# Attention scores of a two-layer decoder trunk as fp32r products of hi and lo parts, query parts stacked on the partitions

## The chip, the cores and the metric

The kernel runs on one core of one Trainium2 chip. The metric is the device time of one execution in microseconds (us), lower is better. "Before" and "after" are the same program but for the change below.

## What is computed

Two decoder layers on x of 256 tokens and 1024 channels. Each layer has a mixing part (this is where the change lies), a cross-attention into a memory of 256 rows, and a feed-forward part that reads 16384 single-neuron experts. Cut to what matters, the attention branch of the mixing part is, for 8 heads of 64 channels in 2 key/value groups of 4 heads:

```python
q = rms_norm(q, q_norm)                                   # (256, 8 heads, 64)
k_s = rms_norm(kv[:, :, 2], k_norm[1]); v_s = kv[:, :, 3] # "selected" branch, (256, 2 groups, 64)
k_w = rms_norm(kv[:, :, 4], k_norm[2]); v_w = kv[:, :, 5] # "window" branch
k_c, v_c = compressed(kv[:, :, 0:2])                      # 15 compressed keys and values per group
for each branch b in (c, s, w):
    o_b = masked_softmax(q @ k_b.T * 64 ** -0.5, causal) @ v_b
o = sum of sigmoid(gate_b) * o_b
```

With 256 tokens the selected and the window branch both see all causal keys, so both are plain causal attention with their own keys and values. Tokens come in two tiles of 128 (t = 0, 1); tile 0 sees 128 keys, tile 1 sees 256.

## The kernel before

**The stream.** All large weights come as "pieces" of 128 rows by 512 columns, 2 to a DMA, in one fixed order. ScalarE (ACT) rounds a piece to fp32r (`w_hi`, line 528), GpSimd (POOL) subtracts to get the rest (`w_lo`, line 494), and TensorE (PE) multiplies: `take(n)` on PE consumes n pieces, each with six fp32r matmuls of 512 columns (hi by hi, hi by lo, lo by hi, for two token tiles; lines 971 to 973). Four slots hold pieces: ACT may fill a slot only when PE has used the piece four before it (`hi(n)` on ACT, semaphore `used`), and POOL follows ACT. The small work of the attention, in plain fp32, is laid between the takes by hand; every engine has its own order written out, joined by semaphores.

**PSUM.** Four banks, `aux`, serve all small work. The list USES (line 90 on) says which use takes which bank in which order. PE waits in `wait_bank_free` for the engine that drains the use before it in that bank, and in `wait_drained` for a drained use; VectorE (DVE) or ACT wait in `wait_filled`.

**Attention.** The keys of both branches are normalised (`knd`), transposed (`kn_T0`, `kn_T1`) and written by DVE at line 1535 into `kTm` with zeros in the other head's half, so that one fp32 matmul gives the scores of a pair of heads; the zeros are four memsets (line 1446). The queries are normalised (line 1521), transposed in pairs of heads (`q_T0`, `q_T1`, 8 transposes in all) and written to `qT` (line 1543). A unit is (t, branch, pair): 16 units, first all of tile 0 and then all of tile 1. For unit u:

- PE `scores(u)`: one fp32 matmul, 256 columns (t = 0) or 512 (t = 1), line 1082. The profile shows an fp32 matmul as two records.
- DVE `unit_scores(u)`: scale and mask (line 1397 holds every `stt`), maximum (line 1615), signal `s_ready`.
- ACT: two exponentials with row sums (line 659), signal `p_exp`; then `hi(2)`, and at units 0, 4, 8 and 12 also `read_gates` (line 572).
- PE, in the loop over units: `take(1)`, wait `p_exp`, transposes `p_T{u}` (line 904; 2 or 4), `scores(u + 2)`, `take(1)`, wait for the drained `p_T{u}`, then 2 or 4 fp32 matmuls with the values (line 1115).
- DVE, in its loop: copy `p_T{u}` (line 1648), `unit_scores(u + 2)`; after every fourth unit `combine` scales the four heads' output by the gate over the sum (lines 1633 to 1640).

The compressed branch: `cmp_s` is eight fp32 matmuls of 32 columns (line 1094) between `scores(1)` and unit 0; DVE masks and exponentiates them in unit 0 (lines 1628, 1629, 1653 to 1655) until `pc_ready`; `oc0` and `oc1` (line 1127) follow in units 2 and 3. Before all this DVE makes the compressed keys: it waits for `cmp_k`, sums squares (line 1418 is the last, signal `kc_mean`), and ACT waits for `kc_mean` between two calls of `hi`.

## Time and profile before

| what | value |
|---|---|
| time, median of 3 runs | 2135.74 us (2135.69 to 2135.74) |
| the profiled execution: its own time | 2134.6 us |
| its span, first to last instruction | 2132.8 us |
| PE busy | 2119.8 us, 99% |
| POOL busy | 1709.4 us, 80% |
| DVE busy | 1227.5 us, 58% |
| ACT busy | 1188.5 us, 56% |
| granted TensorE clock | 1.000 over the whole span |

The trace is of one execution. Times in it count from the first instruction. The units of layer 0 lie at about 115 to 190 us, those of layer 1 about 1059 us later.

In a timeline a row has the start in us, how long until the end in us (for matmuls the end is modelled, and the next one starts before it), engine, line, operation, what it writes and reads, the shape, and how many are merged into the row.

### The profile page before, as it was taken

Reading aid. Unit: us, or ns where it says so; the run is one execution under the profiler, and the core shown is the slowest. Engines: PE = TensorE matmul, PEld = TensorE weight load, DVE = VectorE, ACT = ScalarE, POOL = GpSimd, SP = SyncE. Lnnn points to the kernel's source line nnn. Section 1 sums busy time; section 2 is a strip of 40 time slices with the busy share of each in tenths; the row PEclk is TensorE's granted clock in tenths of the full one; section 3 lists DMA queues with packets and bytes.
Section 4 is the critical chain, followed back from the end, with each engine's and each line's share of the span. In section 5 each row is a group of like instructions: output and inputs, shape, how many; then the busy total and the mean of one; then the engine's idle time right before and its main releaser. Section 6 shows DMA issues by size and latency. Waiting matters only on the chain.

```text
span 2132.8 us, 48901 instructions
## 1 busy us (share of the span) xinstructions
PE 2119.8 (99%) x14774; PEld 1842.0 (86%) x14774; DVE 1227.5 (58%) x2433; ACT 1188.5 (56%) x2287; POOL 1709.4 (80%) x1316
## 2 busy tenths in 40 slices
PE   9999999999999999999999999999999999999999
PEld 7878899999888888888878788999988888888887
DVE  5756448966666555423357564588665666553233
ACT  5555665555555545555555556655555555545565
POOL 7766678888788888888887576798888878888887
PEclk9999999999999999999999999999999999999999
DMA  8433445555544554565574344455555544555555
GB/s 293 157 124 129 147 149 176 179 177 178 166 158 167 168 172 163 196 196 188 188 257 149 123 132 139 154 180 185 178 168 167 167 166 161 173 170 197 189 192 180
DMA packets 101790, 367.87 MB, mean 172 GB/s; under 512 B 11600, under 2 KB 12880, under 8 KB 101456
## 3 DMA queue, kind: packets, MB, share of 16 engines
q1 hardware_dynamic: 97632, 354.46, 50.1%
q10 hardware_dynamic: 4080, 12.42, 1.5%
q8 instruction: 43, 0.70, 0.1%
q14 instruction: 35, 0.29, 0.0%
HBM read 365.78 MB, written 1.05 MB: 172 GB/s over the span
## 4 chain that ended last, share of the span: by engine, by line
PE 96%; DVE 1%; ACT 1%; issue 1%; POOL 1%; DMA 0%; ACTq 0%; DVEq 0%; POOLq 0%
PE acc L1215 11%; PE acc L1301 11%; PE acc L1303 11%; PE acc L1302 11%; PE acc L1205 6%; PE acc L1206 6%; PE acc L1207 6%; PE acc L971 6%; PE acc L973 5%; PE acc L972 5%; PE acc L1214 5%; PE aux L1259 4%; PE aux L904 2%; PE aux L1082 1%; PE aux L1115 1%
## 5 line engine op out<-in xcount | busy, mean ns | idle before, releaser
L494 POOL TENSOR_TENSOR w_lo<-raw,w_hi 128x512 fp32r<-128x512 f32 x1312 | 1709.2, 1314 | 415.6 <-ACT w_hi L528 321.2
L528 ACT ACTIVATE w_hi<-raw 128x512 fp32r<-128x512 f32 x1348 | 843.7, 629 | 651.7 <-PE acc L973 175.1
L1301 PE MATMUL acc<-w_hi,eg 128*128 128x512 f32 x1020 | 401.2, 393 | 0.0
L1303 PE MATMUL acc<-w_hi,eg 128*128 128x512 f32 x1020 | 397.6, 390 | 0.0
L1302 PE MATMUL acc<-w_lo,eg 128*128 128x512 f32 x1020 | 397.1, 389 | 0.0
L1944 DVE TENSOR_TENSOR eg<-big,eg 128x256 fp32r<-128x256 f32 x256 | 159.0, 621 | 398.3 <-ACT eg L785 396.5
L1215 PE MATMUL acc<-h_rows,w_hi 128*128 128x512 f32 x1024 | 355.8, 397 | 0.0
L1205 PE MATMUL acc<-h_rows,w_hi 128*128 128x256 f32 x1024 | 290.5, 284 | 0.0
L1206 PE MATMUL acc<-h_rows,w_hi 128*128 128x256 f32 x1024 | 289.9, 283 | 0.0
L1207 PE MATMUL acc<-h_rows,w_lo 128*128 128x256 f32 x1024 | 289.9, 283 | 0.0
L1214 PE MATMUL acc<-h_rows,w_lo 128*128 128x256 f32 x896 | 249.8, 279 | 0.0
L1303 PEld LDWEIGHTS acc<-w_hi,eg 128*128 128x128 f32 x1020 | 191.5, 188 | 40.5
L1302 PEld LDWEIGHTS acc<-w_lo,eg 128*128 128x128 f32 x1020 | 191.7, 188 | 38.9
L1301 PEld LDWEIGHTS acc<-w_hi,eg 128*128 128x128 f32 x1020 | 191.6, 188 | 38.5
L785 ACT ACTIVATE eg<-big 128x256 fp32r (+1 forms) x256 | 106.8, 418 | 204.4 <-PE acc L1303 204.3
L1215 PEld LDWEIGHTS acc<-h_rows,w_hi 128*128 128x128 f32 x1024 | 185.2, 188 | 33.8
L1205 PEld LDWEIGHTS acc<-h_rows,w_hi 128*128 128x128 f32 x1024 | 196.6, 192 | 0.5
L1207 PEld LDWEIGHTS acc<-h_rows,w_lo 128*128 128x128 f32 x1024 | 196.6, 192 | 0.0
L1206 PEld LDWEIGHTS acc<-h_rows,w_hi 128*128 128x128 f32 x1024 | 196.6, 192 | 0.0
L1214 PEld LDWEIGHTS acc<-h_rows,w_lo 128*128 128x128 f32 x896 | 168.8, 188 | 5.7
L1935 DVE TENSOR_REDUCE big<-acc 128x512 f32 (+1 forms) x128 | 88.5, 692 | 140.4 <-PE acc L1215 140.4
L971 PE MATMUL acc<-w_hi,h_rows 128*128 128x512 f32 x352 | 146.8, 417 | 4.5 <-POOL w_lo L494 1.8
(276 smaller groups left out, 2982.7 us busy)
## 6 DMA issues: line engine op xcount, KB each, us to landing
raw<-stream_dram SPq DMA_DIRECT2D x674, 512.0 KB, 3.3
big<-parb_dram ACTq DMA_DIRECT2D x2, 2128.0 KB, 10.3
big<-mem_dram ACTq DMA_DIRECT2D x2, 1024.0 KB, 5.3
big<-pm_dram ACTq DMA_DIRECT2D x2, 768.0 KB, 15.9
X<-x_dram ACTq DMA_DIRECT2D x1, 1024.0 KB, 8.5
out_dram<-X SPq DMA_DIRECT2D x4, 256.0 KB, 2.1
big<-parr_dram ACTq DMA_DIRECT2D x2, 448.0 KB, 12.0
big<-mem_dram ACTq DMA_DIRECT2D x1, 512.0 KB, 4.9
```

Source lines behind the costliest of these rows:

```text
L494: nc.gpsimd.tensor_tensor(w_lo[:, k % SLOTS, :], raw[:, k // PER_CHUNK, k % PER_CHUNK, :], w_hi[:, k % SLOTS, :].bitcast(F32), ALU.subtrac ...
L528: nc.scalar.activation(w_hi[:, k % SLOTS, :], raw[:, (k // PER_CHUNK) % RAW, k % PER_CHUNK, :], ACT.Copy).then_inc(hi_ready, 1)
L971: pe_.matmul(dst, r_hi[:, kt, ts], w_hi[:, slot, :], start=first, stop=False)
L1205: pe_.matmul(dst, wh, h_hi[:, kt, :], start=(kt == 0), stop=False)
L1206: pe_.matmul(dst, wh, h_lo[:, kt, :], start=False, stop=False)
L1207: return pe_.matmul(dst, w_lo[:, r % SLOTS, wk * P:(wk + 1) * P], h_hi[:, kt, :], start=False, stop=(kt == KD - 1))
L1214: pe_.matmul(acc[:, bank_of, 0:S], w_lo[:, r % SLOTS, at], h_hi[:, kt, :], start=False, stop=False)
L1215: ins = pe_.matmul(acc[:, bank_of, :], w_hi[:, r % SLOTS, at], h_rows[:, kt, :, :], start=(kt == 0), stop=(kt == KD - 1))
L1301: pe_.matmul(dst, eg[:, q % 2, 0, ts], w_hi[:, slot, :], start=start, stop=False)
L1302: pe_.matmul(dst, eg[:, q % 2, 0, ts], w_lo[:, slot, :], start=False, stop=False)
L1303: ins = pe_.matmul(dst, eg[:, q % 2, 1, ts], w_hi[:, slot, :], start=False, stop=stop)
L1944: V.tensor_tensor(eg[:, q % 2, 1, :], src, eg[:, q % 2, 0, :].bitcast(F32), ALU.subtract).then_inc(sig["eg_ready"].sem, 1)
```

## The change

- **Score products.** A unit is now one head with both branches: (g, t, q) for group g, tile t, head q of the group; first all of group 0, then group 1. The query of a head stands twice on the partitions: rows 0 to 63 its fp32r rounding, rows 64 to 127 the rest (`q_ring`, a ring of four). The keys stand twice too, once as rounding and once as rest (`k_parts`). Two fp32r matmuls of 256 or 512 columns then give the sum of all four products. The second token tile of group 1's keys (`k_late`) takes the place of group 0's only after unit 8 (`k_made`).
- **Queries.** Normalised per tile (two instructions in place of one), doubled by ACT (`zq_twice`, two copies of 512 columns), transposed per head (16 transposes in four uses `q_T0` to `q_T3` in place of 8 in two), written to `q_rows` (four instructions in place of two). Per unit DVE makes the parts with `unit_query`: a copy of 128 by 128 and a subtraction on 64 rows. Four are made ahead of `cmp_k`, the others in the loop.
- **Keys.** Per branch three products and two subtractions in place of two products; no zero halves, so the four memsets go.
- **Compressed scores.** Sixteen fp32 matmuls on 64 rows and 16 columns, even heads into one bank and odd into another, in place of eight on 128 rows and 32 columns; DVE drains them with four instructions in place of two.
- **Combination.** Per group and tile, both branches at once; the sum into `ot` becomes two additions of 256 columns where it was one of 512.
- **Banks and order.** The list of bank uses is rearranged, and the query transposes move to four places between the takes.

```diff
+         ("q_T0", 1), ("hid_p", 2), ("pool_d0", 0), ("pool_d1", 3), ("hid", 2), ("zg", 1), ("q_T1", 0), ("cmp_k", 2), ("cmp_v", 3),
+         ("q_T2", 1), ("q_T3", 0), ("mixed", 1), ("pool_y", 0), ("kc_T", 2), ("cmp_s0", 3), ("cmp_s1", 2)]
+UNITS = [(t, g, q) for g in range(KVG) for t in range(T) for q in range(GROUP)]
...
+        q_ring = k_blocks[:, 3, :].rearrange("p (u j) -> p u j", u=4)
...
# ACT, after zg_parts
+                a.wait("qn_ready")
+                for t in range(T):
+                    a.step(nc.scalar.activation(zq_twice[t][:, :, 1, :], zq_twice[t][:, :, 0, :], ACT.Copy), "q_twice" if t else None)
                 hi(2)
...
# PE
                 take(1)
-                e.wait("qn_ready")
-                for i in range(2):
-                    transposes(f"q_T{i}", [zq[:, t, j * P:(j + 1) * P] for j in (2 * i, 2 * i + 1) for t in range(T)])
+                def queries_T(i):
+                    transposes(f"q_T{i}", [zq_twice[t][:, h, :, :].rearrange("p n c -> p (n c)")
+                                           for h in (2 * i, 2 * i + 1) for t in range(T)])
                 take(2)
+                e.wait("q_twice")
+                queries_T(0)
...
                 fill(ins, "zg")
-                take(4)
+                take(2)
+                queries_T(1)
+                take(2)
...
                 fill(pe_.matmul(bank("cmp_v")[:, 0:DK], hid_rep, w2[:, 1, :], start=True, stop=True), "cmp_v")
-                take(4)
+                queries_T(2)
+                take(2)
+                queries_T(3)
+                take(2)
...
                 def scores(u):
+                    e.wait("q_made", u + 1)
+                    if (g, t, q) == (1, T - 1, 0):
+                        e.wait("k_made")
                     e.wait_bank_free(f"s{u}")
-                    fill(pe_.matmul(bank(f"s{u}")[:, 0:2 * w], qT[:, j, t * P:(t + 1) * P], kTm[:, br, j // 2, :, 0:w],
-                                    start=True, stop=True), f"s{u}")
+                    for n in range(2):
+                        keys_at = k_parts[:, n, :, 1 - g:2 - g + t, :]
+                        ins = pe_.matmul(bank(f"s{u}")[:, 0:2 * w], q_ring[:, u % 4, :], keys_at, start=(n == 0), stop=(n == 1))
+                    fill(ins, f"s{u}")
...
+                    for h in range(8):
+                        half = slice((h % 2) * DK, (h % 2 + 1) * DK)
+                        at = t * 64 + (h // 2) * 16
+                        ins = pe_.matmul(bank(f"cmp_s{h % 2}")[:, at:at + 16], q_rows[half, h, t * P:(t + 1) * P],
+                                         kc_rows[half, h // GROUP, :], start=True, stop=True)
...
# DVE
-                for br in range(2):
-                    for h in range(2):
-                        d.step(V.memset(kTm[(1 - h) * DK:(2 - h) * DK, br, :, h, :], 0.0))
...
+                    for g, c in ((0, slice(0, 2)), (1, slice(0, 1))):
+                        src = v[:, g].rearrange("p (c j) -> p c j", c=2)[:, c, :]
+                        hi, lo = (k_parts[:, n, br, 1 - g:1 - g + c.stop, :] for n in range(2))
+                        d.step(V.tensor_scalar(hi, src, gain, None, ALU.mult))
+                        d.step(stt(lo, src, gain, hi.bitcast(F32), ALU.mult, ALU.subtract))
+                    d.step(V.tensor_scalar(k_late[:, br, :], v[:, 1, P:2 * P], gain, None, ALU.mult), drains=use)
+                def query_rows(i):
+                    use = f"q_T{i}"
+                    d.wait_filled(use)
+                    d.step(V.tensor_scalar(q_rows[:, 2 * i:2 * i + 2, :], ..., col[:, C_QN:C_QN + 1], None, ALU.mult), drains=use)
+                def unit_query(u):
+                    t, g, q = UNITS[u]
+                    src, dst, low = q_rows[:, GROUP * g + q, t * P:(t + 1) * P], q_ring[:, u % 4, :], slice(DK, P)
+                    d.step(V.tensor_copy(dst, src))
+                    d.step(V.tensor_tensor(dst[low], src[low], dst[low].bitcast(F32), ALU.subtract), "q_made")
+                query_rows(0)
...
# after the copies of pool_d0 and pool_d1, ahead of cmp_k
+                query_rows(1)
+                for u in range(4):
+                    unit_query(u)
                 d.wait_filled("cmp_k")
...
                        "kcd_ready")
+                query_rows(2)
+                query_rows(3)
...
                     if u + 2 < len(UNITS):
                         unit_scores(u + 2)
+                    if u + 4 < len(UNITS):
+                        unit_query(u + 4)
+                    if u == len(UNITS) // 2:
+                        hi, lo = (k_parts[:, n, :, 1, :] for n in range(2))
+                        d.step(V.tensor_copy(hi, k_late))
+                        d.step(V.tensor_tensor(lo, k_late, hi.bitcast(F32), ALU.subtract), "k_made")
...
+                    for br in range(2):
+                        d.step(V.tensor_tensor(dst, dst, tmp[:, t, br * S:(br + 1) * S], ALU.add), done if br else None)
```

## Rows read from the trace of the kernel before

**Rows 1.** The page: shares of the chain that ended last, by engine.

```profile
PE 96%; DVE 1%; ACT 1%; issue 1%; POOL 1%; DMA 0%; ACTq 0%; DVEq 0%; POOLq 0%
```

**Rows 2.** Windows, the units of layer 0: busy us and instructions per engine, granted clock.

```profile
115.20:188.00 72.80, 72.74 (x377) 57.57 (x377) 37.87 (x73) 41.25 (x106) 41.11 (x32) 1.00 0.35 116
```

**Rows 3.** Timeline of PE: an fp32 score product of each width, and the stream behind.

```profile
119.50 0.60 PE L1082 MATMUL aux<-big 128*128 128x256 f32 x2
...
120.17 0.40 PE L972 MATMUL acc<-w_lo,eg 128*128 128x512 f32 x1
...
121.34 0.55 PE L1115 MATMUL aux<-big 128*128 128x64 f32 x4
...
144.93 1.02 PE L1082 MATMUL aux<-big 128*128 128x512 f32 x2
...
146.02 0.39 PE L972 MATMUL acc<-w_lo,h_rows 128*128 128x512 f32 x1
```

**Rows 4.** Timeline of PE, fp32r products of 256 columns, feed-forward stage, ten apart.

```profile
320.12 0.28 PE L1207 MATMUL acc<-h_rows,w_lo 128*128 128x256 f32 x1
...
321.32 0.28 PE L1205 MATMUL acc<-h_rows,w_hi 128*128 128x256 f32 x1
```

**Rows 5.** Timeline of PE: the eight query transposes, and the stream behind them.

```profile
86.64 1.04 PE L904 MATMUL aux<-cst,big 128*128 128x128 f32 x8
...
87.75 0.39 PE L972 MATMUL acc<-w_lo,eg 128*128 128x512 f32 x1
```

**Rows 6.** Timeline of PE: compressed scores on 128 rows; key products on 64 rows.

```profile
116.10 1.87 PE L1094 MATMUL aux<-big 128*128 128x32 f32 x16
117.81 0.47 PE L971 MATMUL acc<-w_hi,eg 128*128 128x512 f32 x1
...
309.50 2.06 PE L1244 MATMUL aux<-big 64*128 64x128 f32 x32
311.49 0.39 PE L1205 MATMUL acc<-h_rows,w_hi 128*128 128x256 f32 x1
```

**Rows 7.** Three DVE lines with all inputs in SBUF: duration ns min/median/max.

```profile
L1520 DVE TENSOR_TENSOR big<-big,st x8: 461/1397/1399, 79.0 to 1141.4; 128x256 f32<-128x256 f32 x8
L1480 DVE COPY big<-big x4: 1401/1402/1403, 61.9 to 1122.4; 128x512 f32<-128x512 f32 x4
L1640 DVE TENSOR_TENSOR big<-big x8: 691/1130/1295, 137.5 to 1253.1; 128x512 f32<-128x512 f32 x8
```

**Rows 8.** Timeline of DVE, units 0 and 1, and of PE: values of unit 1.

```profile
118.08 0.62 DVE L1397 SCALAR_TENSOR_TENSOR big<-aux,cst 128x128 f32<-128x128 f32 x2 [1.25 <-PE aux L1094]
...
120.55 0.42 DVE L1648 COPY big<-aux 128x256 f32<-128x256 f32 x1
...
122.90 0.73 DVE L1655 TENSOR_SCALAR st<-st 128x16 f32<-128x16 f32 x1
123.75 0.42 DVE L1648 COPY big<-aux 128x256 f32<-128x256 f32 x1
...
125.31 0.55 PE L1115 MATMUL aux<-big 128*128 128x64 f32 x4
```

**Rows 9.** Timeline of POOL: the second piece of unit 0.

```profile
122.31 1.29 POOL L494 TENSOR_TENSOR w_lo<-raw,w_hi 128x512 fp32r<-128x512 f32 x1 [0.18 <-ACT w_hi L528]
```

**Rows 10.** Timeline of DVE, then ACT, ahead of the units: keys, the mean, the next pieces.

```profile
87.54 3.10 DVE L1535 TENSOR_SCALAR big<-aux,col 64x512 f32<-64x512 f32 x4
...
101.25 0.14 DVE L1418 TENSOR_SCALAR st<-st 32x1 f32<-32x1 f32 x1
...
105.64 1.67 ACT L528 ACTIVATE w_hi<-raw 128x512 fp32r<-128x512 f32 x3
109.64 0.63 ACT L528 ACTIVATE w_hi<-raw 128x512 fp32r<-128x512 f32 x1 [2.32 <-PE acc L973]
```

**Rows 11.** Timeline at the end of the units: the last addition; PE's next transposes.

```profile
194.04 1.29 DVE L1640 TENSOR_TENSOR big<-big 128x512 f32<-128x512 f32 x1
...
196.22 1.03 PE L904 MATMUL aux<-cst,big 128*128 128x128 f32 x8
```

More of the change, by code:

```diff
@@ L91 @@
 USES += [("mk_T0", 0), ("mk_T1", 1), ("zg_p", 2), ("raw_T0", 0), ("raw_T1", 1), ("kn_T0", 3), ("kn_T1", 0),
-         ("q_T0", 1), ("q_T1", 2), ("hid_p", 3), ("zg", 3), ("hid", 2), ("pool_d0", 0), ("pool_d1", 1), ("cmp_k", 2), ("cmp_v", 3),
-         ("mixed", 0), ("pool_y", 1), ("kc_T", 2), ("cmp_s", 3)]
-UNITS = [(t, br, j) for t in range(T) for br in range(2) for j in range(PAIRS)]
+         ("q_T0", 1), ("hid_p", 2), ("pool_d0", 0), ("pool_d1", 3), ("hid", 2), ("zg", 1), ("q_T1", 0), ("cmp_k", 2), ("cmp_v", 3),
+         ("q_T2", 1), ("q_T3", 0), ("mixed", 1), ("pool_y", 0), ("kc_T", 2), ("cmp_s0", 3), ("cmp_s1", 2)]
+GROUP = 4
+UNITS = [(t, g, q) for g in range(KVG) for t in range(T) for q in range(GROUP)]
 USES += [("s0", 0), ("s1", 1)]
@@ L1089, in _ @@
                 e.wait_drained("kc_T")
-                e.wait_bank_free("cmp_s")
+                e.wait_drained("q_T3")
+                e.wait_bank_free("cmp_s0")
+                e.wait_bank_free("cmp_s1")
                 for t in range(T):
-                    for j in range(PAIRS):
-                        at = t * P + j * 32
-                        ins = pe_.matmul(bank("cmp_s")[:, at:at + 32], qT[:, j, t * P:(t + 1) * P], KcB[:, j // 2, :, :],
-                                         start=True, stop=True)
-                fill(ins, "cmp_s")
-                for u, (t, br, j) in enumerate(UNITS):
+                    for h in range(8):
[3 more added lines that the diff above has]
+                                         kc_rows[half, h // GROUP, :], start=True, stop=True)
+                        if t == T - 1 and h >= 6:
+                            fill(ins, f"cmp_s{h % 2}")
+                for u, (t, g, q) in enumerate(UNITS):
                     if u == len(UNITS) - 1:
@@ L1102, in _ @@
                     e.wait("p_exp", u + 1)
-                    transposes(f"p_T{u}", [sring[:, u % 2, h, c * P:(c + 1) * P] for h in range(2) for c in range(t + 1)])
+                    transposes(f"p_T{u}", [sring[:, u % 2, br, c * P:(c + 1) * P] for br in range(2) for c in range(t + 1)])
                     if u + 2 < len(UNITS):
@@ L1107, in _ @@
                     e.wait_drained(f"p_T{u}")
-                    use = f"o{u // PAIRS}"
-                    if j == 0:
+                    use = f"o{u // GROUP}"
+                    if q == 0:
                         e.wait_bank_free(use)
-                    for h in range(2):
+                    for br in range(2):
                         for c in range(t + 1):
-                            at = (2 * j + h) * DK
-                            g = j // 2
-                            ins = pe_.matmul(bank(use)[:, at:at + DK], pT[:, u % 2, h * (t + 1) + c, :],
+                            at = (GROUP * br + q) * DK
+                            ins = pe_.matmul(bank(use)[:, at:at + DK], pT[:, u % 2, br * (t + 1) + c, :],
                                              zkv[:, c, 3 + 2 * br, g * DK:(g + 1) * DK], start=(c == 0), stop=(c == t))
-                    if j == PAIRS - 1:
+                    if q == GROUP - 1:
                         fill(ins, use)
@@ L1442, in _ @@
                 rows_norm(ssx, X, xn, "xn_ready")
-                for br in range(2):
-                    for h in range(2):
-                        d.step(V.memset(kTm[(1 - h) * DK:(2 - h) * DK, br, :, h, :], 0.0))
                 halves = ident.rearrange("p (c a n) -> p c a n", c=2, a=2)
@@ L1629, in _, with combine, combine_group @@
                 d.step(V.tensor_tensor(scf, scf, cmb, ALU.subtract), "cs_ready")
-                def combine(use, t, k, weights, first, done=None):
+                def combine(use, shares, weights, dst):
                     d.step(V.reciprocal(coef, weights))
-                    d.step(stt(coef, ng[:, t, k:24:3], 1.0, coef, ALU.add, ALU.mult))
+                    parts = coef if len(shares.shape) == 2 else coef.rearrange("p (b q) -> p b q", b=2)
+                    d.step(stt(parts, shares, 1.0, parts, ALU.add, ALU.mult))
                     d.wait_filled(use)
-                    dst = (ot if first else tmp)[:, t, :].rearrange("p (h c) -> p h c", h=8)
-                    d.step(V.tensor_tensor(dst, bank(use).rearrange("p (h c) -> p h c", h=8),
+                    d.step(V.tensor_tensor(dst.rearrange("p (h c) -> p h c", h=8), bank(use).rearrange("p (h c) -> p h c", h=8),
                                            coef.unsqueeze(2).broadcast_to((P, 8, DK)), ALU.mult), drains=use)
-                    if not first:
-                        d.step(V.tensor_tensor(ot[:, t, :], ot[:, t, :], tmp[:, t, :], ALU.add), done)
+                def combine_group(n, done):
+                    g, t = n // T, n % T
+                    shares = ng[:, t, 3 * GROUP * g:3 * GROUP * (g + 1)].rearrange("p (q k) -> p k q", k=3)[:, 1:3, :]
+                    combine(f"o{n}", shares, sums[:, n % 2, :], tmp[:, t, :])
+                    dst = ot[:, t, g * GROUP * DK:(g + 1) * GROUP * DK]
+                    for br in range(2):
+                        d.step(V.tensor_tensor(dst, dst, tmp[:, t, br * S:(br + 1) * S], ALU.add), done if br else None)
                 unit_scores(1)
                 d.wait_drained("zg")
-                for u, (t, br, j) in enumerate(UNITS):
+                for u, (t, g, q) in enumerate(UNITS):
                     use = f"p_T{u}"
```

88 lines of the change are left out of this document (40 added, 48 removed).

## The prediction, made before the changed kernel was built or timed

> **What bounds the kernel now.** I read the page first: PE is busy for 99% of the span, and the chain that ended last is PE for 96% [rows 1]. Then the stretch of the change itself, the units of layer 0: PE is busy in 72.74 of 72.80 us at a granted clock of 1.00 (2.4 GHz), while DVE works 37.87, ACT 41.25 and POOL 41.11 us [rows 2]. So PE sets the end here, every us that PE is spared is gained, and every us that it is made to wait is lost, as nothing later gives it back. The other engines have 30 us of room in 73, which says little: what counts is whether DVE has each single thing ready when PE comes for it. A busy sum of PE does not price an instruction, since matmuls overlap in the records; I use distances from start to start.
>
> **What it removes from PE.** Behind an fp32 score product of 256 columns the take's second matmul starts 0.67 us after the product's start, behind one of 512 columns 1.09 us [rows 3]. One stream matmul lies between, which costs 0.234 (from 120.17 to 121.34 are five of them [rows 3]). So the products cost 0.67 - 0.23 = 0.43 and 1.09 - 0.23 = 0.86 us. The new ones are two fp32r products each. One of 512 columns is the stream's own kind, 0.23; one of 256 columns costs 0.120 (ten in 1.20 us [rows 4]). A unit of tile 0 then takes 0.24 in place of 0.43, one of tile 1 0.46 in place of 0.86. Eight of each per layer: 8 x 0.19 + 8 x 0.40 = 4.7 us less.
>
> **What it adds to PE.** Eight query transposes more per layer. Eight of them cost 87.75 - 86.64 - 0.23 = 0.88 us [rows 5]; I price four groups of four like two of eight. So 0.9 us more. Compressed scores: eight fp32 matmuls (16 records) took 117.81 - 116.10 = 1.71 us on all rows; 16 on half the rows, even and odd heads by turns as here, took 311.49 - 309.50 = 1.99 us for 32 records in the feed-forward part [rows 6]. The columns are fewer (16 against 128), but the 128 weight columns are the same. I take 0.1 more. Bounds: nothing, and, if the two halves did not run side by side, another 1.7. Values and probability transposes keep their number and size. Net on PE: -4.7 + 0.9 + 0.1 = -3.7 us per layer, if nobody waits.
>
> **What it adds to DVE, and why that is the question.** The trace shows DVE held up by POOL. L1520 has 256 columns and takes 0.46 us at best and 1.40 in the median, L1480 (a copy of 512) 1.40 each time, L1640 (512) 0.69 at best and 1.30 at worst [rows 7]. L1655 works on 16 columns and takes 0.73 us, until 123.63; POOL's subtraction ended at 123.60 [rows 8, 9]. So a DVE instruction whose inputs are all in SBUF, copy, scaling or two-input, may wait for POOL's running subtraction of 1.3 us; then, when POOL has the next piece ready, each of a row of them waits again. Copies and scalings from PSUM in the same stretch do not (0.42 at 120.55 and 123.75 [rows 8]). The added instructions are of the first kind: `unit_query` is an SBUF copy (about 0.22) and a subtraction of 128 columns (about 0.29; both estimates go by 0.42 for 256 columns less the part that grows), 16 times per layer, each up to 1.3 longer; `k_made` is two more, and the second addition in `combine` one more.
>
> The Trainium skill (SBUF — State Buffer, Who interferes with whom) says the same more sharply: the port pair that DVE and GpSimd share is an exclusive lock, taken by fp32 copies in SBUF and by two SBUF inputs, not by a reduction or a lone input outside such a mode. The trace agrees (1.40 against 0.46 in L1520). Were the rule idle here, the sum would be the first rival's.
>
> Now the places in order.
>
> *Ahead of the units.* DVE's work on the keys, 3.10 us for four [rows 10], becomes per branch two instructions of 256 and three of 128 columns from PSUM, some 0.48 and 0.35 each (0.75 for 512 columns, 0.42 for 256 as a copy), so 4.3 us: 1.2 later. `pool_d0` waits for the bank that this drains; in between PE has two more pieces but four fewer transposes. I count 0.2 there, and 0.1 at the bank that `q_T1` takes from `pool_d0`; bounds 0 and 1.5. ACT's two copies (0.63 each, as for a piece) fall where ACT runs ahead. The four `unit_query` before `cmp_k` take 2.3 us alone, and two or three of the eight meet a subtraction, so `kc_mean` comes at about 104.5 in place of 101.4 [rows 10], and the pieces that ACT makes behind it are up to 3.1 late. The three at 105.64 are followed by 2.32 us in which ACT waited for PE [rows 10], and PE comes 0.9 later by its transposes: 3.2 of room. Cost about 0.1.
>
> *Units 0 and 1.* DVE has no gap from 118.08 to the copy at 120.55 [rows 8], and PE starts unit 0's values at 121.34 [rows 3]: the copy had 0.37 us of room. Now PE is there 0.38 earlier after `scores(0)`, 0.19 more after `scores(2)`; DVE drains the compressed scores with four instructions of half the size in place of two of 0.31, +0.4, but starts 0.38 earlier. Wait about 0.3. Then `unit_query(4)` goes in front of the mask products and L1655. POOL's two pieces of unit 0 lie right there (122.31 to 123.60 [rows 9]), so its two instructions take about 1.7 in place of 0.5. Copy 1 came at 123.75 and PE used it at 125.31 [rows 8], 1.1 of room; DVE is now 1.7 later by this while PE arrives 0.5 sooner, net of the first wait. Wait about 1.0; bounds 0 and 2.2.
>
> *Unit 3.* Two combinations meet, and group 0's next units are of tile 1, so masks are 512 wide. `unit_query(7)`, the two additions and the 0.69 copy of `p_T4` end some 0.2 after PE asks; up to 2 if POOL stands in the way. Units 7, 8 (with `k_made`) and 11 have 0.5 us or more left. `k_made` itself is asked for two units later.
>
> *End of the units.* The last addition ran 194.04 to 195.33, and PE came at 196.22 [rows 11]. Two additions of 256, each behind a subtraction of POOL, end at about 196.5: 0.3.
>
> Waits per layer: 0.4 + 0.3 + 1.0 + 0.2 + 0.3 = 2.2 us. Memsets: they end before DVE waits for products of PE, and the way to the mix rows then goes over ACT; 0.
>
> **Sum.** (-3.7 + 2.2) = -1.5 per layer, -3.0 for two. The profiled execution took 2134.6 us by its own time (1.8 more than its span), 1.1 below the median of the runs; the difference applies to either. 2135.74 - 3.0 = 2132.7; with the rounding of the parts I say 2132.6 us, 0.15% faster, which a measurement of this kernel (about 0.2%, 4.3 us) can hardly tell from no change.
>
> **Rivals.**
> 1. *The waits are hidden* (0.25). DVE's small instructions fit between POOL's, or the room at the copies is enough. For it: only 41 of 73 us of POOL are taken in the units [rows 2]. Against: the copy of unit 0 had 0.37 us of room and loses more. Then 2 x -3.7: 2128.3.
> 2. *DVE feeds ACT too late* (0.08, the other side). All eight instructions of the four early `unit_query` wait a full subtraction, 10.4 in place of 2.3 us; `kc_mean` comes at 110, ACT holds back the pieces behind it, POOL too, and PE starves for about 5 us, beside the waits counted. 2 x (-3.7 + 2.2 + 5.1) = +7.2: 2142.9. It eats all gain from a delay of the mean of about 7 us on. Against: POOL has only some four pieces to do there, for ACT that waits gives it none, so the holding ends by itself. A milder form, 1 to 3 us per layer here or along the units, gives 2134.5 to 2139 (0.12).
> 3. *Halves of the array do not overlap* for products so short (0.05): +3.4 on the forecast, 2136.0. Against: rows 6.
> 4. *The parts are no cheaper* (0.02): two fp32r products with three-dimensional keys cost what one fp32 product did. Then +1.0 + 2.2 per layer: 2142.1.
>
> **Chances.** The forecast (2130.2 to 2134.5) has 0.48; a third of it lies below 2131.5. Faster by over 0.2%: 0.25 + 0.15 = 0.40. Slower by over 0.2%: 0.08 + 0.02 = 0.10. The rest, 0.50, within. The range takes in rival 1 with its own spread and the milder form of 2 and rival 3: 2128.0 to 2137.5; the forecast's own is 2130.2 to 2134.5.
>
> **What would show it.** Start to start, a score product and its stream matmul should take 0.47 (tile 0) and 0.69 (tile 1) in place of 0.67 and 1.09. The copies of line 1648's successor in units 0 and 1 should end after PE's take, with PE idle 0.3 and 1.0 us before the values and DVE named as releaser; `unit_query` pairs should show durations near 1 us where POOL is busy and 0.2 to 0.3 elsewhere. The distance from `zg_p` to the last query transposes should grow by no more than 2 us. The units of a layer should shrink by about 3 us. I am wrong if PE's idle before values is nil (rival 1), if POOL's subtractions or ACT's pieces come after PE asks in the takes behind `cmp_v` (rival 2), or if the compressed scores take over 2.5 us (rival 3).

## The result, and the profile after

The changed kernel takes 2142.66 us (median of 7 runs, 2141.61 to 2144.83) against 2135.69 for the kernel before on the same chip: ratio 1.0035, 95% interval 1.0025 to 1.0044. It is slower by 7.0 us, where 3.1 less were forecast. The profiled execution took 2142.09 us with a span of 2139.4.

The page of the changed kernel, its busy line and the shares of its chain, to be held against [rows 1]:

```profile
PE 2118.5 (99%) x14822; PEld 1840.0 (86%) x14822; DVE 1263.5 (59%) x2521; ACT 1191.4 (56%) x2291; POOL 1706.8 (80%) x1316
...
PE 90%; DVE 7%; issue 1%; ACT 1%; POOL 0%; DMA 0%; ACTq 0%; DVEq 0%; POOLq 0%
```

DVE had 1% of the chain and has 7%, though it works only 59% of the time. The busy line of PE says 99% in both kernels and does not tell them apart.

The stretch of the units, from the first score product to the last values of layer 0, in windows: first the kernel before, then the changed one. Columns: window, its length, busy us with instructions for PE, PEld, DVE, ACT and POOL, granted clock, DMA share, GB/s.

```profile
115.24:189.84 74.60, 74.54 (x387) 59.13 (x386) 38.96 (x75) 42.07 (x107) 41.91 (x33) 1.00 0.35 117
```

```profile
117.52:192.29 74.77, 71.86 (x403) 57.64 (x402) 53.88 (x106) 42.10 (x107) 41.79 (x33) 1.00 0.35 118
```

PE's busy time fell by 2.7 us and the stretch grew by 0.2, at the same granted clock of 1.00. DVE works 14.9 us more. PE's work did get shorter; it is now idle for 2.9 us, which is all that it saved and a little more. The waits in 115 to 215 us of the changed kernel name the places (engine and line that waits, releaser: us in total, times, longest):

```profile
PEld aux L1139 <- DVE big L1687: 4.4, 5, 1.6
...
PE aux L1139 <- DVE big L1687: 2.0, 2, 1.2
...
PEld aux L913 <- DVE big L1679: 0.6, 1, 0.6
PEld acc L980 <- DVE big L1421: 0.6, 1, 0.6
PE acc L980 <- DVE big L1421: 0.4, 1, 0.4
PE aux L913 <- DVE big L1669: 0.6, 2, 0.3
```

L1139 is the product with the values, L1687 the copy of `p_T` ahead of it, L913 the transposes, L1669 the draining product of a combination, L1679 its two additions, L1421 every `stt`, here that of the gates. The kernel before has one wait for DVE of 0.2 us in the units. Unit 1 on DVE, where [rows 8] had the copy at 123.75:

```profile
124.39 0.30 DVE L1574 CAST h_rows<-big 128x128 fp32r<-128x128 f32 x1
124.73 1.28 DVE L1575 TENSOR_TENSOR h_rows<-big,h_rows 64x128 fp32r<-64x128 f32 x1
126.04 0.43 DVE L1698 TENSOR_TENSOR big<-big,cst 128x256 f32<-128x256 f32 x1
...
126.96 0.78 DVE L1700 TENSOR_SCALAR st<-st 128x16 f32<-128x16 f32 x1
127.77 0.43 DVE L1687 COPY big<-aux 128x256 f32<-128x256 f32 x1
```

The subtraction of `unit_query(4)` ended at 126.01; a pair of POOL's pieces ran from 123.32 to 125.85. Counted from the first score product of each kernel (115.24 and 117.52), the copy comes 1.7 us later than before. Then unit 3, the largest wait of all, on DVE:

```profile
138.22 0.23 DVE L1574 CAST h_rows<-big 128x128 fp32r<-128x128 f32 x1
138.48 0.29 DVE L1575 TENSOR_TENSOR h_rows<-big,h_rows 64x128 fp32r<-64x128 f32 x1
138.80 0.20 DVE L1665 RECIPROCAL st<-st 128x8 f32<-128x8 f32 x1
139.04 1.14 DVE L1421 SCALAR_TENSOR_TENSOR st<-big,st 128x8 f32<-128x8 f32 x1
140.21 0.69 DVE L1669 TENSOR_TENSOR big<-aux,st 128x512 f32<-128x512 f32 x1
...
141.18 0.17 DVE L1421 SCALAR_TENSOR_TENSOR st<-big,st 128x8 f32<-128x8 f32 x1
...
142.11 1.84 DVE L1679 TENSOR_TENSOR big<-big 128x256 f32<-128x256 f32 x2
143.99 0.69 DVE L1687 COPY big<-aux 128x512 f32<-128x512 f32 x1
```

and on POOL and PE at the same time:

```profile
138.86 1.29 POOL L499 TENSOR_TENSOR w_lo<-raw,w_hi 128x512 fp32r<-128x512 f32 x1 [1.24 <-ACT w_hi L533]
141.92 1.29 POOL L499 TENSOR_TENSOR w_lo<-raw,w_hi 128x512 fp32r<-128x512 f32 x1 [1.76 <-ACT w_hi L533]
```

```profile
141.05 0.63 PE L913 MATMUL aux<-cst,big 128*128 128x128 f32 x4 [0.29 <-DVE big L1669]
...
144.73 1.10 PE L1139 MATMUL aux<-big 128*128 128x64 f32 x8 [1.20 <-DVE big L1687]
```

`unit_query(7)` itself takes an undisturbed 0.52. But it pushes the 8-column `stt` of the combination to 139.04, just behind the start of POOL's piece (138.86 to 140.15), and the `stt` ends at 140.18: 1.14 us for 8 columns, while the next one, at 141.18, where POOL stands still, takes 0.17. The transposes of `p_T4` wait for the bank behind it, and the values of unit 4 for a copy that stands behind two combinations and two additions. Unit 1 shows the cost of an instruction held up; unit 3 that of a small one shifting its neighbours.

The trace split by stages gives a ledger. Each number is how much longer PE takes between two of its instructions than between the same two in the kernel before (starts paired by their order). "Ahead" runs from 75.0 us of the kernel before to the first score product, "units" to the last values, "end" to the stream behind the next transposes (200.06), "merges" to 350.12; then three of these for layer 1. The first column, up to 75.0 us, is mostly the scatter of single executions: in the three runs that leave this part's code as before, e7, e8 and e11, it is -0.03, -0.72 and +0.93, and the largest, +3.33 of e10, belongs to an execution that took 2.6 us more than the median of its runs. A share of it that the change causes is not excluded for the other runs.

```
                           to 75 | layer 0: ahead  units   end  merges | layer 1: ahead  units   end
changed kernel             +0.62 |          +1.67  +0.17  +1.03  +0.34 |          +1.67  +0.17  +1.02
e1  no unit_query          +0.25 |          +1.70  -3.83  +1.01  +0.39 |          +1.63  -3.95  +1.03
e2  unit_query last        +0.63 |          +1.63  -2.31  +1.03  +0.47 |          +1.67  -2.43  +1.01
e3  fp32 product           +0.60 |          +1.71  +3.77  +1.03  +0.45 |          +1.66  +3.61  +1.03
e4  first four late        +0.64 |          +1.19  +0.19  +1.01  +0.39 |          +1.18  +0.16  +1.01
e5  additions deferred     +0.31 |          +1.63  -3.11  +1.03  +0.42 |          +1.64  -3.24  +1.02
e6  reordered              +0.39 |          +1.18  -3.07  +0.84  +0.39 |          +1.18  -3.20  +0.84
e7  old + unit_query       -0.03 |           0.00  +1.31   0.00  +0.10 |           0.00  +1.24   0.00
e8  old + reductions       -0.72 |           0.00  +0.80   0.00  +0.06 |           0.00  +0.78   0.00
e9  three addends          +0.74 |          +1.19  -3.07  +0.88  +0.39 |          +1.17  -3.23  +0.81
e10 keys first             +3.33 |          +2.61  -2.73  +0.88  +0.07 |          +2.61  -3.23  +0.81
e11 old, two additions     +0.93 |           0.00  +1.14  +1.04  +0.07 |           0.00  +1.12  +1.01
e12 copy of part moved     +1.35 |          +1.17  -3.11   0.00  +0.38 |          +1.18  -3.23   0.00
e13 one addition           +0.18 |          +1.63  -0.83   0.00  +0.11 |          +1.63  -1.00  +0.03
e14 neither                +0.15 |          +1.66  -4.09  +0.01  +0.04 |          +1.70  -4.23   0.00
e15 spread                 +1.66 |          +1.18  -4.09  +0.01  +0.33 |          +1.19  -4.20   0.00
```

The two layers agree within 0.2 us everywhere but in the units of e10 (0.5): what happens here repeats with the order of the instructions and is hardly chance.

### The profile page after: what moved, and what is told of

It reads as the page before. It is cut to its first block, busy times and chain, and to the rows that moved or that the text cites. A ratio compares the mean times of both kernels' runs of the same rounds, so it can differ in the third digit from the quotient of the medians.

```text
span 2139.4 us, 49129 instructions
## 1 busy us (share of the span) xinstructions
PE 2118.5 (99%) x14822; PEld 1840.0 (86%) x14822; DVE 1263.5 (59%) x2521; ACT 1191.4 (56%) x2291; POOL 1706.8 (80%) x1316
## 3 DMA queue, kind: packets, MB, share of 16 engines
HBM read 365.78 MB, written 1.05 MB: 171 GB/s over the span
## 4 chain that ended last, share of the span: by engine, by line
PE 90%; DVE 7%; issue 1%; ACT 1%; POOL 0%; DMA 0%; ACTq 0%; DVEq 0%; POOLq 0%
PE acc L1239 11%; PE acc L1325 11%; PE acc L1327 11%; PE acc L1326 11%; PE acc L1229 6%; PE acc L1230 6%; PE acc L1231 6%; PE acc L1238 5%; PE aux L1283 4%; PE acc L980 4%; PE acc L982 4%; PE acc L981 4%; PE aux L913 2%; PE acc L940 1%; PE aux L1139 1%
## 5 line engine op out<-in xcount | busy, mean ns | idle before, releaser
L1988 DVE TENSOR_TENSOR eg<-big,eg 128x256 fp32r<-128x256 f32 x256 | 150.7, 589 | 406.1 <-ACT eg L794 404.3
```

The costliest lines, as they stand in the source:

```text
L1988: V.tensor_tensor(eg[:, q % 2, 1, :], src, eg[:, q % 2, 0, :].bitcast(F32), ALU.subtract).then_inc(sig["eg_ready"].sem, 1)
```

## The experiments

My theory was that DVE's added small instructions wait for POOL, or push others behind it, and PE waits for DVE. Against it stood: PE's own new work costs more than priced; the loss lies ahead of the units; ACT is fed late (the prediction's rival 2). Each run was timed beside the kernel before; the ratio is to that, with its 95% interval.

### e1, e2, e3, e4: which part of the change costs

e1 leaves out `unit_query` from unit 4 on:

```diff
-                    if u + 4 < len(UNITS):
-                        unit_query(u + 4)
```

> Leaves out the 12 pairs of unit_query from unit 4 on (the score products then read old query parts; PE, ACT and POOL do the same work). Theory, DVE's small SBUF instructions are pushed behind POOL's subtractions and PE waits for what follows them: the waits of about 4.2 us per layer inside the units go, the two additions of each combination and what is late ahead of the units stay, so 2142.7 - 2 x 3.5 = about 2135.7 us (2134 to 2138), and the 8-column instruction of combine falls from 1.13 back to about 0.2 us in units 2 and 3. Rival, the loss lies in PE's own new work or in the stages ahead of the units: within 1 us of 2142.7.

Measured 2133.55 us, 0.9991 [0.9982, 1.0000]: 9.1 less than the changed kernel, 2 below the theory's figure and just below its range. The units fell by 4.0 and 4.1 us; ahead and end did not move. The three 8-column `stt` of units 2 and 3 take 0.17 us each here, as expected.

e2 moves the same two lines behind the combinations, at the end of a unit:

> The same DVE instructions, but unit_query comes at the end of each unit, behind the combinations, in place of ahead of them. Theory: the waits for bank 2 at units 2, 3 and 4 (0.18, 0.46 and 0.45 us per layer) go, as combine's 8-column instruction stands again where POOL is idle; the waits for the copies of units 1 and 4 (0.97 and 1.35) stay about as they are, since the sum of DVE's work between two copies is the same. So about 1 to 1.5 us per layer, 2140.0 us (2139 to 2141.5). Rival, only the amount of DVE's work counts and not its place: 2142.7 within 0.5. Rival, the copy suffers more as unit_query now stands right ahead of it: 2144 or more.

Measured 2138.06 us, 1.0018 [1.0009, 1.0027], 4.6 less than the changed kernel with the same instructions, and 0.9 below the expected range. The three waits for bank 2 went as expected, and that of unit 1 too, which I had expected to stay; that of unit 4 stayed and grew from 1.35 to 1.68. DVE in e2, at the place of unit 1:

```profile
124.37 0.49 DVE L1696 TENSOR_TENSOR big<-big,cst 128x256 f32<-128x256 f32 x1
...
125.35 0.69 DVE L1698 TENSOR_SCALAR st<-st 128x16 f32<-128x16 f32 x1
126.08 0.23 DVE L1574 CAST h_rows<-big 128x128 fp32r<-128x128 f32 x1
126.34 0.29 DVE L1575 TENSOR_TENSOR h_rows<-big,h_rows 64x128 fp32r<-64x128 f32 x1
126.66 0.42 DVE L1687 COPY big<-aux 128x256 f32<-128x256 f32 x1
```

The same work between the same two copies now ends 1.1 us earlier, since the pair starts between two of POOL's pieces (one ends at 126.01, the next starts at 126.41). The idea that only the sum between two copies counts was wrong: the order changes the sum.

e3 makes the scores one fp32 product and leaves the keys' low parts out:

```diff
-                    for n in range(2):
-                        keys_at = k_parts[:, n, :, 1 - g:2 - g + t, :]
-                        ins = pe_.matmul(..., q_ring[:, u % 4, :], keys_at, start=(n == 0), stop=(n == 1))
+                    keys_at = k_parts[:, 0, :, 1 - g:2 - g + t, :].bitcast(F32)
+                    ins = pe_.matmul(..., q_ring[:, u % 4, :].bitcast(F32), keys_at, start=True, stop=True)
```

> Each unit's scores are one fp32 product (query parts against the keys' high parts, the keys' low parts left out) in place of two fp32r products; all else stays. Prediction's price of the parts: 8 x 0.19 + 8 x 0.40 = 4.7 us per layer more of PE, of which the units where PE waits for DVE now take back up to 4; theory: +5 to +8 us, 2148 to 2151 us. Rival, the parts are no cheaper than the fp32 product: 2142.7. Rival, the gain was all swallowed by waits at DVE (PE's speed does not matter in the units): also near 2143.

Measured 2150.16 us, 1.0070 [1.0057, 1.0084], 7.5 more than the changed kernel; in the units +3.6 and +3.4 of the 4.7 priced. So the cheaper products are worth most of their price even beside the waits, and rival 4 falls.

e4 puts the first four `unit_query` behind `query_rows(3)`:

> The four early unit_query come behind query_rows(3), not ahead of the compressed keys. Theory (units hold most of the loss): bank 1 comes free earlier for the mixed product, where PE now waits some 0.4 us, and kc_mean returns from 105.0 to about 101.5 us; 0.3 to 0.6 us per layer, 2142.7 - 0.9 = 2141.8 us (2141 to 2142.7). Rival 2 of the prediction in its milder form, ACT held back by the late kc_mean is what costs: 2 us per layer or more, 2138.7 or below.

Measured 2141.22 us, 1.0029 [1.0018, 1.0040], 1.4 less. Ahead of the units 0.48 us per layer came back, where `mixed` (L1079) had waited for the bank that `query_rows(2)` drains; that wait is gone in e4. The mean of the compressed keys was ready 2.8 us earlier, but it was no feeding of ACT that came back: in the changed kernel ACT waited 2.00 us for the mean of the compressed keys, and still had 1.62 us in which it waited for PE:

```profile
105.19 0.20 ACT L659 ACTIVATE st<-st 32x1 f32<-32x1 f32 x1 [2.00 <-DVE st L1442]
...
111.92 0.63 ACT L533 ACTIVATE w_hi<-raw 128x512 fp32r<-128x512 f32 x1 [1.62 <-PE acc L982]
```

### e7, e8, e11: one added cost at a time, in the kernel before

e7 adds to the kernel before, at the place of `unit_query`, only

```diff
+                    if u + 4 < len(UNITS):
+                        qs, qd = qT[:, u % 4, 0:P], spare[:, u % 4, :]
+                        d.step(V.tensor_copy(qd, qs))
+                        d.step(V.tensor_tensor(qd[DK:P], qs[DK:P], qd[DK:P].bitcast(F32), ALU.subtract))
```

> The kernel BEFORE with 12 idle pairs per layer at the place where the changed kernel has unit_query: a copy of 128 columns and a subtraction of 128 columns on half the rows, into a buffer that nobody reads. Nothing else of the change. Theory (DVE's small two-sided SBUF instructions wait for POOL's subtractions, and PE then waits for DVE): PE is slower in these units by 4.7 us per layer than in the changed kernel, so less is late, but about 2.5 us per layer remain, 2135.2 + 5 = 2140 us (2138 to 2142), with pairs of 0.3 to 1.3 us. Rival, DVE has room for them and the loss has its cause elsewhere in the change: 2135.2 to 2136.

e8 has two `tensor_reduce` of 128 columns there instead:

> The kernel BEFORE with 12 pairs of idle reductions per layer at the same place, 128 columns each, about 0.29 us each and so 0.58 for a pair against 0.52 for an undisturbed unit_query. Theory, the waiting for POOL is what costs and a reduction of one input does not wait: each takes its 0.3 us also beside a running subtraction, and the time stays within 1 us per kernel of the kernel before, 2135.2 to 2136.5 us. Rival, the amount and number of DVE's instructions is what costs: as much as the run with the copies and subtractions.

Measured: e7 2138.16 us, 1.0015 [1.0006, 1.0024]; e8 2137.44 us, 1.0010 [1.0001, 1.0019]. Per layer 1.3 and 0.8 us in the units. So e7 lost half of the figure that I expected, at the lower edge of its range, and e8 more than I allowed: its expectation fell. The groups by line (busy us, mean ns) show that the reductions themselves never waited (all at 0.29), while some copies and subtractions did (0.23 and 0.29 alone); first e7, then e8:

```profile
L1654 DVE CAST h_rows<-big 128x128 fp32r<-128x128 f32 x12 | 4.8, 398 | 0.4
L1655 DVE TENSOR_TENSOR h_rows<-big,h_rows 64x128 fp32r<-64x128 f32 x12 | 4.5, 377 | 0.4
```

```profile
L1653 DVE TENSOR_REDUCE st<-big 128x1 f32<-128x128 f32 x12 | 3.4, 286 | 0.4
L1654 DVE TENSOR_REDUCE st<-big 128x1 f32<-128x128 f32 x12 | 3.4, 286 | 0.4
```

But the reductions shifted what follows them. In e8 the mask product of unit 0 started beside POOL's piece (121.60 to 122.89), and the 16-column instruction beside the next:

```profile
121.53 0.29 DVE L1654 TENSOR_REDUCE st<-big 128x1 f32<-128x128 f32 x1
121.85 1.32 DVE L1657 TENSOR_TENSOR big<-big,cst 128x256 f32<-128x256 f32 x1
...
123.66 1.12 DVE L1659 TENSOR_SCALAR st<-st 128x16 f32<-128x16 f32 x1
124.82 0.42 DVE L1648 COPY big<-aux 128x256 f32<-128x256 f32 x1
```

0.58 us of work that is never held made the copy late by more than a microsecond, through its neighbours. But e8's loss is 0.6 of e7's, so the two runs alone do not tell how much of e7's comes from instructions held themselves and how much from shifted ones. The Trainium skill (SBUF — State Buffer, Who interferes with whom) says that a reduction never contends on this chip, and an instruction with two inputs in SBUF does while GpSimd reads SBUF; the trace agrees (the reductions at 0.29 on the mean, the subtraction of e7 at 0.29 alone and 1.34 at worst), and the rule alone would have called e8 harmless.

e11 cuts each addition of a combination in the kernel before into two of 256 columns:

```diff
-                        d.step(V.tensor_tensor(ot[:, t, :], ot[:, t, :], tmp[:, t, :], ALU.add), done)
+                        for n in range(2):
+                            cs = slice(n * S, (n + 1) * S)
+                            d.step(V.tensor_tensor(ot[:, t, cs], ot[:, t, cs], tmp[:, t, cs], ALU.add), done if n else None)
```

> The kernel BEFORE with each of the four additions of a layer's combinations (512 columns) cut into two of 256, as the changed kernel has them; nothing else. Theory: in the last one the second addition waits for one more of POOL's subtractions, 2.47 in place of 1.29 us, the gates come that much later, and PE loses 0.3 at o_ready and 0.6 at the gates; the three others hide. 2135.4 + 2 x 0.95 = 2137.3 us (2136.5 to 2138.3). Rival, the end of the units has room: 2135.4 within 0.5.

Measured 2139.94 us, 1.0023 [1.0014, 1.0032]: 4.5 us more than the kernel before, over twice what I expected. The end cost 1.0 as I had said, but the units 1.1 as well, all of it at one place, the copy of unit 4: two additions of 256 columns took 1.90 us there.

```profile
138.48 1.90 DVE L1642 TENSOR_TENSOR big<-big 128x256 f32<-128x256 f32 x2
140.41 0.42 DVE L1650 COPY big<-aux 128x256 f32<-128x256 f32 x1
```

### e13, e14: how the loss splits in the changed kernel

The old kernel with the pairs alone lost 2.7 us, but the changed kernel gained 9.1 without them. e13 leaves out the second addition:

```diff
-                    for br in range(2):
-                        d.step(V.tensor_tensor(dst, dst, tmp[:, t, br * S:(br + 1) * S], ALU.add), done if br else None)
+                    d.step(V.tensor_tensor(dst, dst, tmp[:, t, 0:S], ALU.add), done)
```

> The changed kernel without the second of the two additions in each of the four combinations of a layer (the selected branch's share is left out). Theory, from the run of the old kernel with two additions, which lost 1.1 us per layer at unit 4 and 0.9 at the end: 2 x (0.9 + about 1.0) less, 2142.7 - 3.8 = 2138.9 us (2137.9 to 2139.9). Rival, unit_query alone causes the waits of the changed kernel and the additions nothing: 2142 or more.

and e14 leaves out this and `unit_query` from unit 4 on, as in e1:

> Both left out: unit_query from unit 4 on and the second additions. Theory, DVE's added instructions in the units make the whole gap to the prediction's first rival, but for 0.7 us per layer ahead of the units: net of PE -3.7, ahead +0.7, first copy +0.2, late in the merges +0.3, so 2135.4 - 2 x 2.5 = 2130.4 us (2129.5 to 2132). Rival, PE's own price was wrong by 1 us per layer or more: 2132.5 or more.

Measured: e13 2137.50 us, 1.0010 [1.0001, 1.0019]; e14 2131.13 us, 0.9983 [0.9974, 0.9992]. Against e14, in the units of a layer (mean of the two): pairs alone (e13) +3.2, additions alone (e1) +0.3, both +4.3; at the end the additions cost 1.0, the pairs nothing. e13 came 1.4 lower than I expected and below its range, e14 within its range. The parts do not add up: 0.8 us per layer come from their meeting, as at the copy of unit 4, 0.9 in e13, 0.15 in e1, 1.35 with both.

### e5, e6, e9, e10, e12, e15: the same instructions in other places

e5 is e2 with the additions of group 0 and `unit_query(7)` behind the copy of unit 4:

```diff
                     if u + 2 < len(UNITS):
                         unit_scores(u + 2)
+                    if u == 4:
+                        add_group(0, None)
+                        unit_query(7)
```

> As the run with unit_query last, and the two additions of group 0 and unit_query(7) come behind the copy and the scores of unit 4. Theory: what is left inside the units is the wait of 1.7 us per layer for the copy of p_T4, which in that run stood behind 0.88 of additions and 1.5 of unit_query; it goes, so 2138.1 - 3.2 = 2134.9 us (2134 to 2136). Rival, the wait has its cause in the two combinations that meet there (oc1 and o0), not in what was added: 2137 or more, the wait stays above 1 us.

Measured 2134.94 us, 0.9998 [0.9989, 1.0007]. The wait of 1.7 at unit 4 went; against e14 about 1.0 stayed per layer, nearly all of it ahead of the scores of unit 7 and the values of unit 5.

e6 adds e4's move, and ends the last combination with a reduction of the two branches and one addition:

> The last one, and the four early unit_query behind query_rows(3), and in the last combination of a layer one of the two additions is a reduction over the two branches (one input, into a free buffer). Theory, the places add up: 2134.9 - 1.4 for the early four - 2 x 0.4 for the end of the units = 2132.7 us (2131.5 to 2134), below the kernel before, as the prediction's net of PE (-3.7 us per layer) says once the waits are gone, less the 0.7 us per layer ahead of the units that stay. Rival, the loss only moves to the next place: 2134.9 or more.

Measured 2134.12 us, 0.9996 [0.9987, 1.0005], worse than its figure: the reduction took 0.71 us, but the single addition behind it 1.54, so the end gave back only 0.2 of 1.0 per layer.

e9 has no addition at the end. The compressed part is copied beside the place of the product, and one reduction sums three:

```diff
+                        d.step(V.tensor_reduce(dst, three.rearrange("p (b x) -> p x b", b=3), AX.X, ALU.add), done)
```

> As the reordered version, but the last combination of a layer has no instruction with two SBUF inputs behind its product: the compressed part is copied early beside the place of the product, and one reduction over three addends (256 outputs of 768 inputs) ends it. Theory: at the end of the units PE loses 0.15 for o_ready and 0.60 for the gates queued behind the last addition, which waited 1.54 us for POOL; the reduction takes about 1.0 and waits for nothing, so both go, and perhaps the 0.3 us late in the merges: 2 x 0.75 to 2 x 1.0 less, 2134.1 - 1.8 = 2132.3 us (2131.5 to 2133.2). Rival, the gates are late by themselves and not because of the additions: 2133.8 or more.

Measured 2134.08 us, 0.9993 [0.9984, 1.0002]: nothing gained. The early copy stood at the last unit ahead of the rows that PE's stream reads next, and PE stood 0.86 us there; the wait had only moved.

e12 makes that copy a unit earlier, at unit 14, where DVE is idle for 3.8 us, with the three addends in the ring of the scores:

> As the version with three addends, but the compressed part is copied at unit 14, where DVE idles for 3.8 us, into the free scores ring, and no longer ahead of the copies of the branch rows, where it cost PE 0.86 us per layer. Theory: that wait goes and nothing takes its place, 2134.1 - 2 x 0.86 = 2132.4 us (2131.7 to 2133.2), faster than the kernel before by 0.15%. Rival, something else at the end of the units ends last and takes it back: 2133.8 or more.

Measured 2132.92 us, 0.9991 [0.9982, 1.0000], 0.5 above its figure. The end is at 0.00 in both layers. DVE in e12:

```profile
192.73 0.69 DVE L1669 TENSOR_TENSOR big<-aux,st 128x512 f32<-128x512 f32 x1
193.46 1.05 DVE L1684 TENSOR_REDUCE big<-big 128x256 f32<-128x768 f32 x1
194.54 2.85 DVE L1421 SCALAR_TENSOR_TENSOR big<-big,acc 128x512 f32<-128x512 f32 x4
```

The reduction reads 768 columns in 1.05 us in a stretch in which POOL works on four pieces without a break (192.91 to 197.95); the two additions of 256 took 2.47 in the changed kernel.

e10 is e9 with the layer norm's statistics (1.55 us) behind the keys:

> The same, and the five instructions of the layer norm's statistics (1.55 us) come behind the work on the keys instead of ahead of it. Theory: pool_d0 now waits 0.4 us per layer for the bank that the last key instruction drains; with the keys 1.55 earlier it waits no more, 2 x 0.4 less: 2131.5 us. Rival: ACT, which takes the root of these statistics in its order, comes 3 us later with pieces of weights, and PE starves: 2132.3 or more.

Measured 2136.62 us, 1.0006 [0.9997, 1.0015], 2.5 worse than e9, so the rival: ahead +2.6 in place of +1.2. The waits of 75 to 125 us in e10 show ACT behind DVE, and PE behind the copies of `pool_d`:

```profile
PEld aux L913 <- DVE big L1593: 1.9, 1, 1.9
ACT st L598 <- DVE st L1575: 1.9, 1, 1.9
```

e15 is e12 with the additions of group 0 at unit 6 in place of unit 4 (`if u == 6: add_group(0, None)`):

> As the best version so far, but the two additions of group 0 come behind the scores of unit 8, where DVE then idles for 2.2 us, and no longer between the copies of units 4 and 5, where five instructions behind POOL took 3.4 us and the copy of unit 5 came 0.7 us late. Theory: 2 x 0.7 less, 2132.9 - 1.4 = 2131.5 us (2130.5 to 2132.3). Rival, the waits only move to another copy: 2132.9 within 0.5.

Measured 2131.09 us, 0.9978 [0.9968, 0.9987]: faster than the kernel before, by 4.2 us, and 11.6 below the changed one, with the whole change in it, only in another order and with the last two additions made one reduction. Its units, in the window from the first score product to the last values:

```profile
118.08:188.60 70.52, 70.46 (x403) 57.83 (x402) 52.37 (x107) 42.10 (x107) 42.32 (x33) 1.00 0.37 124
```

DVE works 52.4 us there, 11.5 more than in e14, which takes 70.51 for the same stretch. With the order right, `unit_query` and the additions cost PE nothing in the units and at their end: the ledger has -4.09 and 0.01 for layer 0 in both runs.

## Why the prediction was wrong, point by point

**What bounds.** Right: PE sets the end, DVE decides by single things being ready. The share of DVE in the chain, 1% to 7%, is the sign of it.

**PE's price.** Nearly right. Between the values of units 0 and 1 PE takes 3.80 us in e14 and 3.97 before, so a product of tile 0 saves 0.17 (said 0.19). From the last stream matmul ahead of four transposes to the values behind them, with a product of tile 1 between, PE takes 2.52 us in unit 4 of e14 and 2.92 in units 11 and 12 before, so 0.40 (said 0.40). The direct distance I named, in the changed kernel, product to second stream matmul, is 0.55 (121.62 to 122.17) and 0.77 (141.44 to 142.21) and not 0.47 and 0.69; the part of the saving that this hides lies ahead of the product. Compressed scores took 119.98 - 118.08 = 1.90 us, 0.19 more than before (said 0.1) and far from the 2.5 named for rival 3, which falls. With the 0.17 that PE waits for the copy of unit 0 in e14 too (said 0.3), the units of e14 fell by 4.2 where the forecast has -4.7 + 0.1 + 0.3 = -4.3.

**Ahead of the units.** Said 0.9 + 0.4, measured 1.67 per layer. What stays of it in e4, 1.19, is the eight transposes (0.9 as priced) and a wait of 0.3 at `pool_d0` (said 0.2). The step that I missed is `mixed`, 0.4 to 0.5: its bank is now drained by `query_rows(2)`, which stands behind the compressed keys, which stand behind four `unit_query`. e4 gave back 0.48.

**Rival 2.** Its time, 2142.9, is 0.2 from the result, by a mechanism that did not happen; that is luck. `kc_mean` came at 105.0 us, within half a microsecond of what I said, and ACT had room left.

**The step that failed** is "Waits per layer: 0.4 + 0.3 + 1.0 + 0.2 + 0.3 = 2.2 us", in two of its terms and in places that it does not have. The start-to-start distances of PE in layer 0 of the changed kernel, each less the 0.23 of its last stream matmul, give: copy of unit 0 0.17 (said 0.3), of unit 1 0.97 (1.0), of unit 4 1.35 (0.2, "Unit 3", with up to 2 if POOL stood in the way, which it did); transposes of `p_T2`, `p_T3` and `p_T4` 0.18, 0.46 and 0.45, which I did not have; copies of units 8 and 12 0.29 and 0.28, which I had called covered. In sum 4.15 against 1.5. The end, 0.3, measured 1.03: 0.34 at the transposes, and 0.6 at the stream behind them, which waits for the gates that stand behind the additions:

```profile
199.01 1.09 PE L913 MATMUL aux<-cst,big 128*128 128x128 f32 x8 [0.18 <-DVE big L1679]
200.46 0.50 PE L980 MATMUL acc<-w_hi,h_rows 128*128 128x512 f32 x1 [0.35 <-DVE big L1421]
```

From start to start that is 1.45 us, and 0.80 in the kernel before (196.22 to 197.02). I followed the addition only to the next wait of PE and not to what is queued behind it on DVE.

For both layers, forecast to result: waits in the units 2 x 2.7 = 5.3, end 2 x 0.7 = 1.4, ahead 2 x 0.4 = 0.7, PE's price in the units about 0.5, merges 0.3. That is 8.2 of 10.1. Of the rest 0.6 lies in the first 75 us of this one execution and about 0.7 is spread over the units in amounts under 0.1 us each. Another 0.9 lies outside the span, where the sum had nothing: a run's own time is 1.8 us above its span in every run of the kernel before that has its span on record, and 2.5 to 2.8 above it in the seven of the changed kernel (median 2.7). The prediction carried the difference of the spans over to a run's own time, as if this margin stayed the same; it did not, and what makes it grow is open. In turn 0.5 goes off, since the two profiled executions differ by 7.5 us and the medians by 7.0. The prediction's range reached 2137.5, as it allowed at most 3 us per layer for late copies and took unit 1 for the worst place; a slowdown of over 0.2% had a chance of 0.10.

**Why unit 3 was missed.** I priced each added instruction as alone or held up, and did not move the ones behind it. `unit_query(7)` cost 0.52 there and the 8-column `stt` behind it 1.14 in place of 0.17. In e8 even instructions that are never held up did this. The reading that DVE waits for POOL was right. Its other half, that copies from PSUM do not, was drawn from two rows during which POOL mostly stands still; it holds by the whole trace, where all 32 copies of L1648 take 0.42 to 0.69 us by their size.

**Still open.** The 0.3 to 0.5 us in the merges of layer 0 (near 264 us, a rounding by ACT that comes later) stand in the changed kernel and in all its versions but e10, e13 and e14, and not in layer 1; I did not find what sets them. How late a shift must be to meet a piece of POOL was only read from timelines, not varied in steps, and no run took POOL's subtractions away.

## What to carry to other kernels

When small instructions are added to an engine whose instructions can be held until a busy neighbour's end, lay out its whole row of instructions anew against the neighbour's timeline, up to the next thing that the bounding engine waits for: the added time is often the least of it, the shift of those behind is what costs. Before giving up on such a change, move the added work to where the trace shows the engine idle; here the same instructions in other places made 7.0 us slower into 4.2 us faster. And follow each delayed result past its own consumer, to what is queued behind it on the same engine.

## What had not been expected of the hardware

- An instruction of 8 columns can take 1.14 us, and one of 16 columns 1.12, beside a subtraction of POOL of 1.3; the one of 8 columns takes 0.17 elsewhere. Beside POOL the size of such an instruction does not tell its duration.
- Cutting one addition of 512 columns (1.29 us at the end of the units) into two of 256 cost 1.2 us more there (2.45), since the second waits for one more piece; a reduction over three addends of 256 did all of it in 1.05.
- In the first 75 us, where the code of e7, e8 and e11 is that of the kernel before, single profiled executions differ by up to 1.7 us, and e10's began 3.3 late; differences between two profiles have to be taken stage by stage.
